# An attention step's value products are taken at the head of the next step, ahead of its scores

## The reference, cut to what matters

```python
BRANCHES = ((128, 1), (512, 4), (2048, 16))

def dilated_attention_mixer(x, positions, k_sh, v_sh, w_q, w_o):
    q = (x @ w_q).reshape(B, S, N_BRANCHES * N_HEADS, HEAD_DIM)
    q = rope(q, positions).reshape(B, S, N_BRANCHES, N_HEADS, HEAD_DIM)
    for g, (window, dilation) in enumerate(BRANCHES):
        o, lse = dilated_branch(q[:, :, g], k_sh[:, :, g], v_sh[:, :, g], window, dilation)
        ...
    wts = jax.nn.softmax(jnp.stack(lses, axis=0), axis=0)
    o = jnp.einsum("gbsh,gbshd->bshd", wts, jnp.stack(outs, axis=0))
    return o.astype(x.dtype).reshape(B, S, N_HEADS * HEAD_DIM) @ w_o
```

## Time and profile before

| | |
|---|---|
| median of three runs | 1116.43 us (1116.19 to 1117.71) |
| the profiled execution's own time | 1117.65 us |
| its span | 1115.6 us |
| TensorE (PE) busy | 1100.5 us, 99% of the span |
| weight load (PEld) busy | 998.2 us, 89% |
| DVE busy | 755.4 us, 68% |
| ACT busy | 593.3 us, 53% |
| mean granted TensorE clock | 0.998 |
| matmuls of scores, values, turned probabilities | lines 819, 845, 834: 2%, 2%, 1% of the chain that ended last |

### The profile page before, as it was taken

How to read it: one execution, slowest core, us unless ns; L and a number is a source line. 1 busy time by engine, 2 the same in 40 slices (tenths; PEclk the granted TensorE clock), 3 DMA queues, 4 the chain that set the end, 5 groups by cost and what they waited for, 6 DMA issues and landing times.

```text
span 1115.6 us, 18330 instructions
## 1 busy us (share of the span) xinstructions
PE 1100.5 (99%) x6820; PEld 998.2 (89%) x6820; DVE 755.4 (68%) x1161; ACT 593.3 (53%) x871; POOL 54.6 (5%) x47
## 2 busy tenths in 40 slices
PE   7999999999999999999999999999999999999998
PEld 6997888888999999999978888888999989999987
DVE  6976755564686676766657555655777687989970
ACT  6436654453645555553567454644446656656640
POOL 0100000000000000000000000000020011122210
PEclk9999999999999999999999999999999999999999
DMA  8554756666495545452246656682626564655670
GB/s 275 187 179 154 245 169 199 234 216 199 130 230 157 164 130 152 125 157 75 95 122 190 203 172 223 212 262 59 199 83 200 159 220 124 188 180 188 227 245 19
DMA packets 215670, 193.75 MB, mean 174 GB/s; under 512 B 9609, under 2 KB 190909, under 8 KB 215613
## 3 DMA queue, kind: packets, MB, share of 16 engines
q1 hardware_dynamic: 215401, 192.88, 55.7%
q10 hardware_dynamic: 212, 0.09, 0.0%
HBM read 191.88 MB, written 1.05 MB: 173 GB/s over the span
## 4 chain that ended last, share of the span: by engine, by line
PE 96%; DVE 1%; ACT 1%; DMA 1%; SPq 0%; issue 0%; DVEq 0%; ACTq 0%
PE ps L665 14%; PE ps L667 14%; PE ps L666 14%; PE ps L610 8%; PE ps L611 8%; PE ps L612 8%; PE ps L764 6%; PE ps L766 6%; PE ps L765 6%; PE ps L819 2%; PE ps L845 2%; PE ps L834 1%; PE ps L853 1%; PE ps L679 1%; PE ps L713 1%; PE ps L677 1%
## 5 line engine op out<-in xcount | busy, mean ns | idle before, releaser
L1643 DVE TENSOR_TENSOR w_lo<-raw,w_hi 128x1024 fp32r<-128x1024 f32 (+1 forms) x298 | 398.6, 1382 | 57.2 <-ACT w_hi L1207 56.8
L1207 ACT ACTIVATE w_hi<-raw 128x1024 fp32r<-128x1024 f32 (+1 forms) x298 | 331.1, 1156 | 123.8 <-PE ps L667 34.1
L610 PE MATMUL ps<-x_hi,w_hi 128*128 128x256 f32 x656 | 186.7, 285 | 0.0
L612 PE MATMUL ps<-x_hi,w_lo 128*128 128x256 f32 x656 | 185.6, 283 | 0.0
L611 PE MATMUL ps<-x_lo,w_hi 128*128 128x256 f32 x656 | 185.6, 283 | 0.0
L665 PE MATMUL ps<-w_hi,x_hi 128*128 128x512 f32 (+1 forms) x328 | 129.1, 394 | 0.0
L667 PE MATMUL ps<-w_hi,x_lo 128*128 128x512 f32 (+1 forms) x328 | 127.5, 389 | 0.0
L666 PE MATMUL ps<-w_lo,x_hi 128*128 128x512 f32 (+1 forms) x328 | 127.3, 388 | 0.0
L610 PEld LDWEIGHTS ps<-x_hi,w_hi 128*128 128x128 f32 x656 | 125.8, 192 | 1.3 <-issue 1.3
L611 PEld LDWEIGHTS ps<-x_lo,w_hi 128*128 128x128 f32 x656 | 125.9, 192 | 0.0
L612 PEld LDWEIGHTS ps<-x_hi,w_lo 128*128 128x128 f32 x656 | 125.8, 192 | 0.0
(11 more groups left out here) (231 smaller groups left out, 1779.0 us busy)
## 6 DMA issues: line engine op xcount, KB each, us to landing
raw<-in_ffn_w_gate_up SPq DMA_DIRECT2D x176, 256.0 KB, 4.2
raw<-in_w_up SPq DMA_DIRECT2D x44, 512.0 KB, 4.5
raw<-in_ffn_w_down SPq DMA_DIRECT2D x24, 768.0 KB, 5.9
raw<-in_conv_w_in SPq DMA_DIRECT2D x24, 512.0 KB, 5.0
raw<-in_w_q SPq DMA_DIRECT2D x48, 256.0 KB, 4.3
raw<-in_w_kv SPq DMA_DIRECT2D x48, 256.0 KB, 4.3
raw_v<-in_w_kv SPq DMA_DIRECT2D x48, 256.0 KB, 4.2
raw<-in_w_in SPq DMA_DIRECT2D x20, 512.0 KB, 4.5
```

The lines of the kernel that those rows point to most:

```text
L610: nc.tensor.matmul(o, wh[:, k0 + k, c], hi[:, k, :], start=(k == 0), stop=False)
L612: ins = nc.tensor.matmul(o, wl[:, k0 + k, c], hi[:, k, :], start=False, stop=(k == kt - 1))
L1207: nc.scalar.activation(w_hi[:, s, a * ph.cols:b * ph.cols], src, ACT.Copy)\
L1643: nc.vector.tensor_tensor(w_lo[:, s, c], src, w_hi[:, s, c], ALU.subtract)\
```

## The change

Steps 2 to 8 begin with `value(q - 1)`, the value product of the pair attended in the step before, directly followed by `score` of pair q; only then come `ready` and tile Q0. `value` is gone from behind tile K1. The last pair's value product stays in step 8. Its output moves to columns 256 to 511 of bank 7, the score blocks to banks 3 to 7, with another order of the twelve; the wait for `o_stored` moves from ahead of `score` to ahead of its eleventh matmul. `value` has 12 matmuls, 6 of 256 and 6 of 128 columns, instead of 18 of 128.

ACT copies the output (`store_y`) between the two halves of the V split of the next step. DVE takes the two value stores at the head of the next step, ahead of the maxima, and cuts the V split in two halves that it takes later; `store_v(0)` waits for `head_done`. In step 0 the low split of the next K is now ahead of the value stores, which are the first work of step 1. On ACT and DVE step 1 is taken out of the loop.

```diff
-        S_AT = ((3 * 512, 5 * 512), (4 * 512, 6 * 512 + 256))
-        S_ORDER = ((0, 0, 0), (1, 1, 0), (0, 0, 1), (0, 0, 2), (1, 0, 0), (0, 1, 0), (1, 0, 1), (1, 0, 2), (0, 1, 1),
-                   (1, 1, 1), (0, 1, 2), (1, 1, 2))
+        S_AT = ((6 * 512, 3 * 512), (6 * 512 + 384, 4 * 512 + 256))
+        S_ORDER = ((0, 0, 0), (1, 1, 0), (0, 0, 1), (0, 0, 2), (1, 1, 1), (0, 1, 0), (1, 1, 2), (0, 1, 1), (1, 0, 0),
+                   (0, 1, 2), (1, 0, 1), (1, 0, 2))
+        O_AT = 7 * 512 + 256
...
                 def score():
                     if isinstance(i, int) and i == 1:
                         pe.wait_ge(v_stored, 1)
-                    else:
-                        pe.wait_ge(o_stored, q)
                     pe.wait_ge(qk_stored, q * 4 + 4)
...
-                        if (hh, qt, g) == (0, 1, 2):
-                            pe.wait_ge(bank_scored, q + 1)
+                        if (hh, qt, g) == (1, 0, 0):
+                            pe.wait_ge(bank_scored, q * 2 + 2)
+                        if (hh, qt, g) == (1, 0, 1) and not (isinstance(i, int) and i == 1):
+                            pe.wait_ge(o_stored, q)
...
-                        for kt, qt in ((0, 0), (0, 1), (1, 1)):
+                        for kt in range(2):
...
                 elif tail:
+                    value(q - 1)
                     score()
...
-                    value()
+                    value(q)
                 else:
+                    if not (isinstance(i, int) and i == 1):
+                        value(q - 1)
+                    score()
                     ready(ph, 0, i, bank=False)
-                    pe.wait_ge(qk_stored, i * 4)
                     token_major(ph, 0, 0, banks[0], m_hi, m_lo, signal=1, done=tile_a_done)
-                    score()
...
                     token_major(ph, 1, 1, banks[3], x_hi, x_lo, signal=1)
-                    value()
                     turn(2)
```

ACT, steps 1 to 7 and step 8:

```diff
-                    split(ph, 2, i)
+                    split(ph, 2, i, parts=(0,))
+                    if not (isinstance(i, int) and i == 1):
+                        store_y()
+                    split(ph, 2, i, parts=(1,))
                     exps()
...
                 if tail:
                     split(w_o_, 2, 0)
+                    store_y()
                     exps()
+                    act.wait_ge(o_stored, 7)
+                    nc.scalar.activation(m_hi[:, 6, :], y[:, 6, :], ACT.Copy).then_inc(o_hi, 1)
```

DVE, step 8, step 0 and steps 1 to 7:

```diff
                 if not project:
                     split(w_o_, 2, 0, parts=(0,))
+                    store_v(0)
+                    store_v(1)
                     max_of(0)
                     max_of(1)
                     scale(0)
                     scale(1)
+                    output_low(6, 7)
...
                     split_next(0)
+                    split_next(1)
+                else:
                     store_v(0)
                     store_v(1)
-                    split_next(1)
-                else:
-                    split(ph, 2, i)
-                    rope(i, 0, banks)
                     max_of(0)
                     max_of(1)
+                    split(ph, 2, i, parts=(0,))
+                    rope(i, 0, banks)
                     scale(0)
+                    scale(1)
                     rope(i, 1, banks)
-                    scale(1)
+                    split(ph, 2, i, parts=(1,))
                     split_next(0)
                     rope(i, 2, banks)
...
                     split_next(1)
-                    store_v(0)
-                    if last:
-                        output_low(6, 7)
-                    store_v(1)
```

More of the change, by code:

```diff
@@ L816, in score @@
                         o0 = S_AT[hh][qt] + g * w
-                        if (hh, qt, g) == (0, 1, 2):
-                            pe.wait_ge(bank_scored, q + 1)
+                        if (hh, qt, g) == (1, 0, 0):
+                            pe.wait_ge(bank_scored, q * 2 + 2)
+                        if (hh, qt, g) == (1, 0, 1) and not (isinstance(i, int) and i == 1):
+                            pe.wait_ge(o_stored, q)
                         ins = nc.tensor.matmul(flat[:, o0:o0 + w], qT[f, g, tok(qt)], kT[f, g, 0:w], start=True, stop=True,
                                                skip_group_check=True)
-                        if (hh, qt, g) == (1, 1, 0):
+                        if (hh, qt, g) in ((1, 1, 0), (0, 0, 2)):
                             ins.then_inc(bank_scored, 1)
-                        if (qt, g) == (1, 2):
+                        if (hh, qt, g) in ((0, 1, 2), (1, 0, 2)):
                             ins.then_inc(scored, 1)
@@ L835, in turn_p, with value @@
                     ins.then_inc(prob_turned, 1)
-                def value():
+                def value(q):
                     pe.wait_ge(prob_stored, q + 1)
@@ L840, in value @@
                     for g in range(3):
-                        for kt, qt in ((0, 0), (0, 1), (1, 1)):
+                        for kt in range(2):
                             for hh in range(2):
                                 f = slice(hh * HD, (hh + 1) * HD)
[L844 to L847, removed]
+                                w = T - kt * P
+                                c = PT_AT[hh][kt] + g * w
+                                ins = nc.tensor.matmul(ps[f, 7, 256 + kt * P:512], v_tok[:, kt, g * P + hh * HD:g * P + (hh + 1) * HD],
+                                                       prob[:, c:c + w], start=(g == 0 and kt == 0), stop=(g == 2 and kt == 1),
+                                                       skip_group_check=True)
                     ins.then_inc(head_done, 1)
@@ L1414, in split_next, with store_y @@
                         split(ph, j, i + 1)
+                def store_y():
+                    act.wait_ge(head_done, q)
+                    nc.scalar.activation(y[:, ds(q - 1, 1), :].rearrange("p o t -> p (o t)"), flat[:, O_AT:O_AT + T], ACT.Copy)\
+                        .then_inc(o_stored, 1)
                 if tail:
                     split(w_o_, 2, 0)
+                    store_y()
                     exps()
+                    act.wait_ge(o_stored, 7)
+                    nc.scalar.activation(m_hi[:, 6, :], y[:, 6, :], ACT.Copy).then_inc(o_hi, 1)
                     act.wait_ge(lo_ready, 2 * w_o_.n0)
@@ L1423, in attn_step @@
                     act.wait_ge(head_done, PAIRS)
-                    nc.scalar.activation(m_hi[:, 7, :].rearrange("p (t c) -> p t c", t=2), ps[:, 3:5, 384:512], ACT.Copy)\
-                        .then_inc(o_hi, 1)
+                    nc.scalar.activation(m_hi[:, 7, :], flat[:, O_AT:O_AT + T], ACT.Copy).then_inc(o_hi, 1)
                 elif not attend:
@@ L1442, in attn_step @@
                     split_next(1)
-                    act.wait_ge(head_done, q + 1)
-                    nc.scalar.activation(y[:, ds(q, 1), :].rearrange("p o (t c) -> p (o t) c", t=2), ps[:, 3:5, 384:512],
-                                         ACT.Copy).then_inc(o_stored, 1)
                     store(2)
                     store(3)
-                    if last:
-                        act.wait_ge(o_stored, 7)
-                        nc.scalar.activation(m_hi[:, 6, :], y[:, 6, :], ACT.Copy).then_inc(o_hi, 1)
             def hybrid_part(what, k):
@@ L1538, in emit @@
                     attn_step(0, True, False)
-                    with act.Fori(1, 7) as i:
+                    attn_step(1, True, True)
+                    with act.Fori(2, 7) as i:
                         attn_step(i, True, True)
@@ L1899, in store_v @@
                     if t == 0:
-                        dve.wait_ge(tile_a_done, i * 3 + 3)
-                    else:
-                        dve.wait_ge(product_done, ph.n(3, i) + 1)
-                    nc.vector.tensor_scalar(v_tok[:, t, :], ps[:, banks[4 + t], 0:384], rcol[:, t:t + 1], None, ALU.mult)\
+                        dve.wait_ge(tile_a_done, q * 3 + 3)
+                        if not (isinstance(i, int) and i == 1):
+                            dve.wait_ge(head_done, q)
+                    else:
+                        dve.wait_ge(product_done, ph.n(3, q) + 1)
+                    v_bank = (TILE_BANK_0 if isinstance(i, int) and i == 1 else TILE_BANK)[4 + t]
+                    nc.vector.tensor_scalar(v_tok[:, t, :], ps[:, v_bank, 0:384], rcol[:, t:t + 1], None, ALU.mult)\
                         .then_inc(v_stored if t else va_stored, 1)
@@ L1914, in attn_step @@
                     dve.wait_ge(o_hi, KD)
-                    nc.vector.tensor_tensor(m_lo[:, 7, :].rearrange("p (t c) -> p t c", t=2), ps[:, 3:5, 384:512],
-                                            m_hi[:, 7, :].rearrange("p (t c) -> p t c", t=2), ALU.subtract)\
+                    nc.vector.tensor_tensor(m_lo[:, 7, :], flat[:, O_AT:O_AT + T], m_hi[:, 7, :], ALU.subtract)\
                         .then_inc(o_split, 1)
@@ L2089, in emit @@
                     attn_step(0, True, False)
```

(7 more changed lines are left out.)

## The result

The changed kernel takes 1121.02 us (median of 6 runs, 1120.56 to 1121.56), the kernel before 1116.35 us on the same chip: ratio 1.0039, 95% interval 1.0026 to 1.0052, slower by 0.4%. The forecast was 1121.0 us. The profiled execution took 1120.68 us with a span of 1118.6, 3.0 us more than the 1115.6 of before.

The account below looks back on a forecast made before the run. PE, busy 99% of the span, was taken to bound the kernel. From 1116.3 us, + 4.4 (wait) + 1.7 (clock) - 1.3 (pairs) gave 1121.1; the forecast was 1121.0 us, range 1119.2 to 1123.2.

Parts of the forecast that it names:

- The start of step 1: PE's first scores of step 1 wait for value stores now behind the K split: 4.4 us lost, bounds 4.2 to 4.8.
- The clock: Behind PE's wait at the start of step 1, one stretch at the lower clock: 1.7 us lost, as before.
- the rival of a longer low clock: Two low-clock stretches instead of one behind the wait at step 1's start: 1122.7 us, chance 0.20.
- The pairs: Values directly ahead of scores in steps 2 to 8 save 0.19 us a step, 1.3 us in all, bounds 0.7 to 2.1.
- the prediction's estimate: Some 60 cycles per matmul, six fewer in each of eight pairs: 1.2 us more gained; not counted in the forecast.
- The covers: Copy, value stores, probabilities, turn(2), V load and step 8's stores stay hidden from PE in the loop: each at nothing.
- the 1.2 us to spare: ACT's output copy ends 1.2 us before PE needs it at the eleventh of twelve score matmuls.
- The basis: Sum starts from runs of before near 1116.3 us, taken to be without the clock's fall.

Follow-up runs that it names:

- first experiment: Changed kernel with the two value stores of step 0 back between the low splits of Q and K: 1117.4 us, ratio to before 1.0001.
- values back: Changed kernel with the value product back behind tile K1 of its own step: 1125.94 us, ratio to before 1.0083.
- changed kernel kept busy: Changed kernel with 50 unread transposes of the identity on PE at the end of step 0: 1119.51 us, ratio to before 1.0022.
- stores in Q: Changed kernel with step 0's two value stores between the halves of the low Q split: 1115.01 us, repeated 1115.06 us, ratio to before 0.9984 both times.
- changed kernel again: Changed kernel unaltered, run again on another run's chip: median 1122.36 us, ratio to before 1.0044.
- 18 narrow matmuls: Changed kernel with 18 value matmuls of 128 columns instead of 6 of 256 and 6 of 128: 1121.45 us, ratio to before 1.0043.
- V split whole: Changed kernel with the low split of V uncut and ahead of the maxima on DVE: 1121.83 us, ratio to before 1.0044.
- values back, copy first: Changed kernel with the value product behind tile K1 and ACT's output copy ahead of its V split: 1124.05 us, ratio to before 1.0069.
- wait for the copy in front: Changed kernel with the wait for o_stored ahead of the first score matmul instead of the eleventh: 1126.03 us, ratio to before 1.0083.

## Why the prediction was right

**The start of step 1** was the term that decides, 4.4 us; the trace has 4.33, and moving the stores alone (first experiment) brings the kernel back to the time of before. The order of DVE's code gave the sum, with durations from rows.

**The clock**: one fall behind the wait, for 3.7 us of work, as taken. The stretch itself was twice as long as before, 6.8 us, and the rival of a longer low clock was right in that; it cost no more only because its first half lay in the wait. The first experiment shows the other case. So the reason that I gave (one stretch, as before) was wrong, and that the size came out is partly luck: with the same wait of 6.2 us, seven profiles have between 3.1 and 5.6 us of the low stretch under work, 1.6 to 2.8 us (table at the end), and this one lies near the lower end.

**The pairs**: 0.19 us a step forecast, 0.19 measured between the two kernels, made of 0.14 for the place and 0.04 for the wider matmuls. I had put all 0.19 to the place and nothing to the form; the two misses cancel, both inside the bounds. The fixed cost of a matmul that the page of the Trainium skill (TensorEngine Tiling, Instruction Overhead) names, added for each matmul as the prediction's estimate has it, is not seen here: 0.04 us for six matmuls, not 0.15. The new order of the scores was not run by itself; scores to scores with the values back, 32.92, leave 0.05 us for it and the form together.

**The covers** all held, with no wait of PE in the loop. That of the copy is the one with least behind it: the 1.2 us to spare were some 0.9, an estimate from the run with the values back. There a copy that ended 1.86 us behind the start of the scores was 0.4 late, and in the changed kernel it ends at 394.64, 0.60 us behind it: 1.86 - 0.4 - 0.6.

**The basis.** I took the runs of before near 1116.3 us for runs without the fall of the clock. The clock on record for each run bears that out. Of the 68 runs of before that were timed beside the experiments, 31 have a mean granted clock of 0.998, and all of them take 1117.2 us or more; of the 37 at 0.999 or 1.0, 34 take less than 1117.0, and three 1117.3 to 1117.6. The mean doesn't say where in a run the clock fell; the one profile of before has its fall behind the wait. The other way of adding up avoids the clock: 1116.3 for runs without a fall, + 4.33 - 1.3 = 1119.3 us, and the changed kernel kept busy takes 1119.5.

## What to carry to other kernels

When a loop's order is turned, look at the step where it starts: an instruction moved ahead of the others (scores ahead of the first tile) makes its own wait the first in the queue, and what stood there hidden is now in front of everybody. Here the fix was two stores taken in the middle of the Q split, and it turned a loss of 0.4% into a gain of 0.16%. And before a group is moved, list what runs under it: the values covered a copy, a pair of stores and half a split besides what they computed.

## What the runs showed that I had not expected

The granted clock was low for 3.4 us behind PE's 1.8 us wait in the profile of the kernel before, and for 6.8 us in all eight profiles with a wait of 2.9 or 6.2 us there. Behind waits of 1.2 us (stores in Q, both profiles) it did not fall. What differs from profile to profile is when the low stretch begins, and so how much of it falls under work; half of that is lost (us; in the first seven rows the wait is 6.2 us, in the last 2.9):

| | clock low | PE resumes | low under work | lost |
|---|---|---|---|---|
| changed kernel | 323.5 to 330.4 | 326.7 | 3.7 | 1.8 |
| changed kernel again | 325.3 to 332.2 | 328.2 | 4.0 | 2.0 |
| 18 narrow matmuls | 322.8 to 329.7 | 326.5 | 3.1 | 1.6 |
| V split whole | 323.4 to 330.2 | 326.5 | 3.7 | 1.8 |
| values back | 324.0 to 330.8 | 326.6 | 4.1 | 2.1 |
| values back, copy first | 325.2 to 332.0 | 326.5 | 5.5 | 2.7 |
| wait for the copy in front | 326.4 to 333.3 | 327.6 | 5.6 | 2.8 |
| stores then K | 322.6 to 329.5 | 323.3 | 6.2 | 3.1 |

So a shorter wait can cost more in clock than a longer one, and the price of one and the same wait moves by over 1 us between profiles. The kernel before has two groups of times, near 1116.3 and 1117.6 us, that go with the mean clock; a gain of 1.5 us has to be read beside that, and is read best among runs of the same clock.
